# Two attention mixers of a transformer block, each written as one interleaved program

## The reference

```
h = rms_norm_2(x, n1)
proj = h @ w_in_l
qa, ka, va, qd, kd, vd, qc, kc, vc = jnp.split(proj, cuts, axis=-1)
qa = rms_norm_2(heads(qa, H_NA), qg[0])          # 4 heads: neighbourhood, with a bias
ka = rms_norm_2(heads(ka, H_NA), kg[0])
out_a = neighbourhood_attention(qa, ka, heads(va, H_NA), rpb_l, na_idx, na_dr, na_dc)
qd = partial_rotary(rms_norm_2(heads(qd, H_DIL), qg[1]), cos1, sin1)   # 6 heads: dilated
kd = partial_rotary(rms_norm_2(heads(kd, H_DIL), kg[1]), cos1, sin1)
out_d = dilated_window_attention(qd, kd, heads(vd, H_DIL), dil_idx, dil_val)
qc = axial_rotary(rms_norm_2(heads(qc, H_GQ), qg[2]), cos_r, sin_r, cos_c, sin_c)  # 6 heads on 2: grouped
kc = axial_rotary(rms_norm_2(heads(kc, H_GKV), kg[2]), cos_r, sin_r, cos_c, sin_c)
out_c = gqa_block_attention(qc, kc, heads(vc, H_GKV))
mix = jnp.concatenate([rms_norm_2(out_a, og[:NA_W]), rms_norm_2(out_d, og[NA_W:NA_W + DIL_W]),
                       rms_norm_2(out_c, og[NA_W + DIL_W:])], axis=-1)
return x + mix @ w_out_l
```

## Time and profile before

| | us |
|---|---|
| median of 3 runs | 1798.05 (1797.01 to 1801.28) |
| the profiled execution | 1802.4 |
| its span, first to last instruction | 1800.6 |
| TensorE busy | 1683.3 |
| VectorE busy | 1024.3 |
| ScalarE busy | 844.1 |
| GpSimd busy | 152.2 |

### The profile page before, as it was taken

The page is one execution under the profiler, slowest core; times in us unless marked ns, Lnnn a source line. Parts: engine busy times, 40 slices in busy tenths (PEclk is TensorE's granted clock), DMA queues, the critical chain, the costliest instruction groups (busy, mean ns, idle before and its releaser), DMA issues.

```text
span 1800.6 us, 28794 instructions
## 1 busy us (share of the span) xinstructions
PE 1683.3 (93%) x11689; PEld 1526.4 (85%) x11689; DVE 1024.3 (57%) x1303; ACT 844.1 (47%) x1185; POOL 152.2 (8%) x190
## 2 busy tenths in 40 slices
PE   7999997899999999998999998968999997899998
PEld 7999885799989999886689997946999987579997
DVE  6444555544455444668654445675655566666654
ACT  5344465444435443436544444564544454644443
POOL 0000011000000000230000002530000038000000
PEclk9999997999999999999999999989999998999999
DMA  7555441355545555432045555511545564025452
GB/s 267 187 186 187 162 153 61 133 194 186 186 164 188 185 181 181 154 118 71 25 176 187 183 179 139 201 48 47 187 166 197 182 180 163 1 100 190 177 188 92
DMA packets 40546, 276.85 MB, mean 154 GB/s; under 512 B 5505, under 2 KB 6290, under 8 KB 7570
## 3 DMA queue, kind: packets, MB, share of 16 engines
q1 hardware_dynamic: 39010, 271.00, 42.5%
q0 software_dynamic: 1456, 4.72, 1.7%
HBM read 274.65 MB, written 1.05 MB: 153 GB/s over the span
## 4 chain that ended last, share of the span: by engine, by line
PE 80%; DVE 9%; ACT 5%; POOL 3%; issue 2%; DMA 0%; SPq 0%; POOLq 0%; DVEq 0%; ACTq 0%
PE bank L661 19%; PE bank L642 14%; PE bank L644 14%; PE bank L643 14%; PE bank L622 5%; PE bank L573 3%; PE bank L574 3%; PE bank L575 3%; DVE w_lo L1356 2%; ACT prob L1178 1%; POOL proj L500 1%; ACT work L1064 1%; DVE prob L1536 1%; PE bank L718 1%; ACT w_hi L1054 1%
## 5 line engine op out<-in xcount | busy, mean ns | idle before, releaser
L1356 DVE TENSOR_TENSOR w_lo<-raw,w_hi 128x2048 fp32r<-128x2048 f32 x255 | 587.4, 2308 | 533.9 <-ACT w_hi L1054 533.2
L1054 ACT ACTIVATE w_hi<-raw 128x2048 fp32r<-128x2048 f32 x255 | 487.3, 1917 | 552.2 <-PE bank L644 404.0
L642 PE MATMUL bank<-xt_hi,w_hi 128*128 128x256 f32 x2112 | 599.8, 284 | 5.7 <-DVE xt_lo L1388 5.7
L644 PE MATMUL bank<-xt_hi,w_lo 128*128 128x256 f32 x2112 | 598.2, 283 | 0.0
L643 PE MATMUL bank<-xt_lo,w_hi 128*128 128x256 f32 x2112 | 598.1, 283 | 0.0
L642 PEld LDWEIGHTS bank<-xt_hi,w_hi 128*128 128x128 f32 x2112 | 405.6, 192 | 9.4 <-issue 5.0
L643 PEld LDWEIGHTS bank<-xt_lo,w_hi 128*128 128x128 f32 x2112 | 405.7, 192 | 2.5
L644 PEld LDWEIGHTS bank<-xt_hi,w_lo 128*128 128x128 f32 x2112 | 405.7, 192 | 0.0
L661 PE MATMUL bank<-w_hi,h_hi 128*128 128x512 f32 x528 | 208.3, 395 | 0.2
L661 PE MATMUL bank<-w_hi,h_lo 128*128 128x512 f32 x528 | 208.5, 395 | 0.0
L661 PE MATMUL bank<-w_lo,h_hi 128*128 128x512 f32 x528 | 208.2, 394 | 0.0
(11 more groups left out here) (301 smaller groups left out, 1635.2 us busy)
## 6 DMA issues: line engine op xcount, KB each, us to landing
raw<-in_stream SPq DMA_DIRECT2D x255, 1024.0 KB, 4.9
work<-in_rpb POOLq DMA_DIRECT2D x32, 64.0 KB, 3.7
X<-in_x SPq DMA_DIRECT2D x2, 512.0 KB, 4.0
prob<-in_cmp_w POOLq DMA_DIRECT2D x1, 1024.0 KB, 5.3
O<-in_cmp_w POOLq DMA_DIRECT2D x1, 1024.0 KB, 7.0
out<-X SPq DMA_DIRECT2D x1, 1024.0 KB, 4.0
cst<-in_consts SPq DMA_DIRECT2D x1, 776.0 KB, 5.9
O<-in_final_gain POOLq DMA_DIRECT2D x1, 512.0 KB, 4.2
```

The costliest lines, as they stand in the source:

```text
L642: pe.matmul(o, w_hi[:, sl, cols], xt_hi[:, k, :], start=(k == 0), stop=False)
L644: ins = pe.matmul(o, w_lo[:, sl, cols], xt_hi[:, k, :], start=False, stop=(k == KD - 1))
L1054: act.activation(w_hi[:, sl, :], raw[:, sl, :], ACT.Copy).then_inc(hi_done, 1)
L1356: dve.tensor_tensor(w_lo[:, sl, :], raw[:, sl, :], w_hi[:, sl, :].bitcast(F32), ALU.subtract).then_inc(lo_done, 1)
```

## The change

Each mixer becomes one function `sec_mixer` for each of three engines, in which the stages are interleaved by hand.

- The columns come as grouped, dilated, values of both, neighbourhood. TensorE takes the projection's units in halves of 24 matmuls and puts the attention of the grouped and then the dilated heads between them; steps of the output projection go between the jobs of the last pairs. The projection uses two banks, the output projection four (0 to 3), scores two, the transposed probabilities one, outputs and square sums one. The transposed probabilities have four places in SBUF.
- Sqrt and reciprocal become Ln and Exp with scale -0.5 on ScalarE, with the Newton step kept; the output norms get a Newton step too. The output norm is computed for each kind on its own, three square sums at a time.
- VectorE prepares the first token tile of the grouped and of the dilated heads, GpSimd the second, and both of the neighbourhood heads. GpSimd adds the mask after the dilated heads.
- The shared functions of the other stages lose their branches for the second block.

In the core of the diff, the first `sec_mixer` is TensorE's, the second ScalarE's, the third VectorE's; the last lines are GpSimd's.

```diff
 SEC_W = dict(qa=256, ka=256, va=256, qd=384, kd=384, vd=384, qc=384, kc=128, vc=128)
-SEC_ORDER = ("qa", "ka", "qd", "kd", "qc", "kc", "va", "vd", "vc")
-QA, KA, QD, KDL, QC, KC, VA, VD, VC = (sum(SEC_W[m] for m in SEC_ORDER[:i]) for i in range(9))
+SEC_ORDER = ("qc", "kc", "qd", "kd", "vc", "vd", "qa", "ka", "va")
...
+SEC_FT_BANK = (2, 3, 2, 3, 2, 4, 5)
...
+SEC_KINDS = ((QC, 8, 0, 1, 384), (QD, 12, 8, 4, 384), (QA, 8, 20, 8, 256))
+SEC_S, SEC_T, SEC_O = (4, 5), 6, 7
...
+            def sec_mixer(l):
...
+                def half(c, t):
+                    if t == 0:
+                        pe.wait_ge(lo_done, u0 + c + 1)
+                        if c >= 2:
+                            pe.wait_ge(pj_evac, p0 + c - 1)
+                    sl = (u0 + c) % NSPLIT
...
+                def transposes(g):
+                    if g == 0:
+                        pe.wait_ge(ft_ready_d, 4 + 2 * l)
+                        pe.wait_ge(ft_ready_p, 4 + 3 * l)
+                    elif g == 2:
+                        pe.wait_ge(ft_ready_d, 5 + 2 * l)
+                        pe.wait_ge(ft_ready_p, 5 + 3 * l)
+                        pe.wait_ge(ft_a, a0 + 1)
+                    elif g == 3:
+                        pe.wait_ge(ft_a, a0 + 2)
+                        pe.wait_ge(ft_d, d0 + 1)
+                    elif g == 4:
...
+                    if m in (0, 3, 6):
+                        pe.wait_ge(ft_a, a0 + (2, 3, 4)[m // 3])
+                        pe.wait_ge(ft_d, d0 + (1, 3, 4)[m // 3])
+                    if m == 6:
+                        pe.wait_ge(na_ready, l + 1)
+                    if m:
+                        pe.wait_ge(exp_done, 2 * (j0 + 2 * m))
+                    duo = [(jobs[i], bank[SEC_S[i % 2]]) for i in (2 * m, 2 * m + 1)]
...
+                def turn_p(i):
+                    pe.wait_ge(p_scaled, j0 + i + 1)
+                    if i:
+                        pe.wait_ge(pt_evac, j0 + i)
+                    for n, (qt, kt) in enumerate(pt_blocks(jobs[i])):
...
+                for c in range(5):
+                    half(c, 0)
+                    half(c, 1)
+                transposes(0)
+                transposes(1)
+                half(5, 0)
+                scores(0)
+                half(5, 1)
+                half(6, 0)
+                scores(1)
+                turn_p(0)
+                half(6, 1)
+                turn_p(1)
+                half(7, 0)
+                scores(2)
+                turn_p(2)
+                values(0)
+                turn_p(3)
+                half(7, 1)
+                transposes(2)
+                transposes(3)
+                half(8, 0)
+                transposes(4)
+                scores(3)
+                turn_p(4)
+                values(1)
+                turn_p(5)
+                half(8, 1)
+                scores(4)
+                turn_p(6)
+                values(2)
+                turn_p(7)
+                half(9, 0)
+                square_sums(0)
+                half(9, 1)
+                scores(5)
+                turn_p(8)
+                values(3)
+                turn_p(9)
+                out_k(0)
+                transposes(5)
+                transposes(6)
+                turn_p(10)
+                values(4)
+                turn_p(11)
+                scores(6)
+                out_k(1)
+                values(5)
+                scores(7)
+                square_sums(1)
+                turn_p(12)
+                out_k(2)
+                turn_p(13)
+                turn_p(14)
+                values(6)
+                turn_p(15)
+                out_k(3)
+                values(7)
+                square_sums(2)
+                out_k(4)
+                out_k(5)
+                out_last()
...
+            def sec_mixer(l):
...
+                def head_root(n):
+                    act.wait_ge(e_ms, 3 * l + n + 1)
+                    act.activation(head_rms(rstd, n), head_rms(ms, n), ACT.Ln).then_inc(e_ln, 1)
+                    act.wait_ge(e_ln, 3 * l + n + 1)
+                    act.activation(head_rms(rstd, n), head_rms(rstd, n), ACT.Exp, scale=-0.5).then_inc(e_rt, 1)
...
+                def out_root(kind):
+                    act.wait_ge(e_m, 3 * l + kind + 1)
+                    act.activation(o_norm[:, kind, :], o_ms, ACT.Ln).then_inc(e_ml, 1)
+                    act.wait_ge(e_ml, 3 * l + kind + 1)
+                    act.activation(o_norm[:, kind, :], o_norm[:, kind, :], ACT.Exp, scale=-0.5).then_inc(e_mr, 1)
...
+                evac(0)
+                split(u0 + 3)
+                evac(1)
+                head_squares(0)
+                split(u0 + 4)
+                head_root(0)
+                evac(2)
+                split(u0 + 5)
+                evac(3)
+                split(u0 + 6)
+                evac(4)
+                head_squares(1)
+                tiles(0)
+                tiles(1)
+                split(u0 + 7)
+                head_root(1)
+                exponentials(0)
+                evac(5)
+                split(u0 + 8)
+                turned(0)
+                exponentials(1)
+                evac(6)
+                turned(1)
+                split(u0 + 9)
+                turned(2)
+                exponentials(2)
+                turned(3)
+                pair_out(0)
+                evac(7)
+                tiles(3)
+                split(u0 + 10)
+                turned(4)
+                exponentials(3)
+                turned(5)
+                pair_out(1)
+                evac(8)
+                head_squares(2)
+                split(u0 + 11)
+                turned(6)
+                exponentials(4)
+                turned(7)
+                pair_out(2)
+                head_root(2)
+                evac(9)
+                split(u0 + 12)
+                out_root(0)
+                turned(8)
+                exponentials(5)
+                turned(9)
+                pair_out(3)
+                out_hi(0)
+                out_hi(1)
+                tiles(5)
+                turned(10)
+                turned(11)
+                pair_out(4)
+                exponentials(6)
+                out_hi(2)
+                pair_out(5)
+                split(u0 + 13)
+                turned(12)
+                out_root(1)
+                exponentials(7)
+                turned(13)
+                out_hi(3)
+                turned(14)
+                pair_out(6)
+                turned(15)
+                out_hi(4)
+                out_hi(5)
+                pair_out(7)
+                out_root(2)
+                out_hi(6)
+                out_hi(7)
+                split(u0 + 14)
...
+            def sec_mixer(l):
...
+                def newton(r, q, mean_sq, ins_sem):
+                    link(dve.tensor_tensor(q, r, r, ALU.mult))
+                    link(dve.tensor_tensor(q, q, mean_sq, ALU.mult))
+                    link(dve.tensor_scalar(q, q, -0.5, 1.5, ALU.mult, ALU.add))
+                    ins = dve.tensor_tensor(r, r, q, ALU.mult)
...
+                split(u0 + 3)
+                head_sums(0)
+                split(u0 + 4)
+                head_root(0)
+                sec_heads(dve, link, 0, 0, l, KT[:, 2048:2560])
+                dve.sem_inc(ft_ready_d, 1)
+                split(u0 + 5)
+                split(u0 + 6)
+                tiles(1)
+                head_sums(1)
+                split(u0 + 7)
+                head_root(1)
+                maxima(0)
+                scale(0)
+                maxima(1)
+                sec_heads(dve, link, 1, 0, l, KT[:, 2048:2560])
+                dve.sem_inc(ft_ready_d, 1)
+                split(u0 + 8)
+                scale(1)
+                split(u0 + 9)
+                maxima(2)
+                tiles(2)
+                scale(2)
+                split(u0 + 10)
+                tiles(4)
+                maxima(3)
+                scale(3)
+                head_sums(2)
+                maxima(4)
+                split(u0 + 11)
+                head_root(2)
+                scale(4)
+                out_mean(0)
+                maxima(5)
+                split(u0 + 12)
+                out_root(0)
+                out_scale(0)
+                out_scale(1)
+                scale(5)
+                out_lo(0)
+                out_scale(2)
+                out_lo(1)
+                tiles(6)
+                maxima(6)
+                out_lo(2)
+                scale(6)
+                split(u0 + 13)
+                maxima(7)
+                out_mean(1)
+                out_root(1)
+                out_scale(3)
+                scale(7)
+                out_scale(4)
+                out_lo(3)
+                out_scale(5)
+                out_lo(4)
+                out_lo(5)
+                out_mean(2)
+                out_root(2)
+                out_scale(6)
+                out_scale(7)
+                out_lo(6)
+                out_lo(7)
+                split(u0 + 14)
...
```

(50 more changed lines are left out.)

369 lines of the change are left out of this document (238 added, 131 removed).

## The result

The changed kernel takes 1817.2 us (median; 1815.1 to 1824.1) against 1798.3 us: a ratio of 1.0106, 95% interval 1.0079 to 1.0133. It is slower by 19 us. The forecast was 1808.7 us: right in sign, inside the range, 8.5 us too low.

The account below looks back on a forecast made before the run. TensorE, busy 93%, bounds it; 28 us a mixer of waits and clock were removable. New waits 25.3 + clock 7.3 = 32.6: +4.7 and +5.9 us, so 1798.05 + 10.6 = 1808.7 us; 8-in-10 range 1786 to 1820.

Parts of the forecast that it names:

- first transposes: TensorE's wait for GpSimd's first heads tile, prepared beside VectorE's: tile ready at 31.5 us, TensorE there at 29.1; 2.5 us.
- third job: Wait ahead of its transposes: VectorE's dilated tile, split and scalings, perhaps held by GpSimd's mask; 1.2 to 5.4, taken as 3.3 us.
- ninth and tenth job: Wait put at the tenth job, behind ScalarE's copies, split, two table loads and two passes: 3.9 us.
- first output matmul: Wait at the output projection's start, behind two exponentials, two scalings and the output tile's lower half: 3.9 us.
- fifteenth job: Wait for table loads and passes (3.4 us) and exponentials (1.8) under one output step of 2.7: 4.1 us.
- the later transfer: In the second mixer the transfer that the first roots need comes 1.2 us later, making that mixer +5.9 us.
- The clock: Half clock on TensorE after three or four new long waits, up to 2.8 us each, partly absorbed: 7.3 us a mixer.
- The clock holds: Rival: TensorE keeps full clock through the mixers, only waits remain, 5 us less than now a mixer, 1789 us; 23%.
- One table load serves Ln and Exp: Rival: ScalarE's roots need one load, tenth and fifteenth job come 2.6 us earlier, 1795 us; 8%.
- The interleaving costs more: Rival: coupled queues, whole 4.5 us mask, another clock fall (2.8), slower-draining loads; +11 us a mixer, 1820 us; 14%.
- The forecast case: The likeliest case over both mixers, 1800 to 1816 us by the ends of mask and clock; 45%.
- the stretched dilated tile: Sign named for being right: VectorE's tile of the dilated heads lasts longer where GpSimd's 4.5 us mask runs.

## Why the prediction was right in sign and 8 us short

**The mechanism held.** It said that the ceiling was 28 us of waits and clock a mixer, and that four coupled queues would lose more than that again. They lost 25.3 + 10.0 and 26.8 + 10.5 us. Of the 8.5 us that the forecast was too low, 4.1 lie in the mixers (6.3 and 8.4 us longer, not 4.7 and 5.9) and 3.4 behind them.

**The waits: 25.3 us predicted, 25.3 measured.** That the two agree to the tenth is luck; the sum is better than its terms:

| ahead of | predicted | measured |
|---|---|---|
| first transposes | 2.5 | 0 (and 0.95 behind them, for a split) |
| first and second scores | 0.7 | 0.31 + 0.45 |
| third job | 3.3 | 5.57 |
| fourth scores | 2.3 | 2.15 |
| eighth job, square sums | 2.5 | 1.58 + 0.34 |
| ninth and tenth job | 3.9 | 0.49 + 1.60 + 1.26 |
| first output matmul | 3.9 | 5.39 |
| fifteenth job | 4.1 | 3.90 |
| last place | 2.1 | 0.78 + 0.48 |

- First transposes: GpSimd began 20.3 us in (predicted 20.8) but took 8.7 us, not 10.7, and was done 29.0 us in, not 31.5. The two engines pay less for each other over a row of short instructions than I had read from the earlier trace rows.
- Third job: the step "if it holds VectorE off to its end, all of it counts; if not, nothing; I take the middle" was mis-sized. The earlier trace rows already showed a multiply that ended with GpSimd's (1.96 us long, 1.4 of them beside GpSimd's; no row shows the multiply of 1.40 us that the prediction names); that row decided the case, and the middle between two exclusive ends is a value that neither gives. The multiply lasted 4.84 us, some 4.2 more than the one before it.
- First output matmul: 1.5 us short. VectorE's split of 2.28 us started at 1203.06, 0.4 us after ScalarE's Exp was done, and the correcting passes behind it only at 1205.26.
- Second mixer: the later transfer was put at +1.2 us; the waits grew by 1.5.

**The clock: 7.3 us predicted, 10.0 and 10.5 measured.** This is the largest miss inside the mixers, 5.9 us; 2.3 us of it are made good, since the old mixers held 7.0 and 7.5 us of half clock (124.0 and 124.5 outside the waits) and not 6.1. I let each long wait cost 2.8 us and took off what the next wait absorbs. Shorter waits in a row count too: 0.49, 1.60 and 1.26 us ahead of the ninth to the tenth job left the values at 1.49 us and the next transposes at half clock, and the half clock then lasted through the 5.39 us wait and twelve output matmuls. The runs with filled waits show that the 10 us are clock: without their fillings they take 117 to 118 us in the first mixer.

**Behind the mixer: nothing predicted, 3.4 us measured.** The walk ended at the last output matmul. "SyncE's queue only waits for splits" was looked at; VectorE's order at the seam, split ahead of the update of X, was not.

**The rivals.** "The clock holds" is out: 0.90. With filled waits the clock did hold (0.99), but the time was 1802.6 us and not that rival's 1789. (The "even load of 76%" read for it is 78% in the earlier trace rows.) "One table load serves Ln and Exp" is out: two loads a root in all 12 roots. The Trainium skill's rule (ScalarE: Activation LUTs, section Table sets: the hidden batching unit) doesn't describe this program. The rival's price of 14 us for one load in two was not measured; leaving out 22 of the 24 loads came to 18, which by the load (0.8 us, an estimate) would be about 10 for 12 of them. "The interleaving costs more", with the whole mask and one more fall of the clock, to which I gave 14%, is the nearest to what happened: 1820 against 1817.2; no row shows its third part, loads that drain longer. The forecast case, to 1816, missed by a microsecond.

**The signs.** Of those named ahead, the 12 loads a mixer, the wait of 3.9 us ahead of the fifteenth job, the clock below 0.95 and the stretched dilated tile came true. The wait at the first output matmul, 5.4 us, was above the 3.5 to 4.5 named. GpSimd's first tile was 2.5 us early, and the tenth job waited 1.26 us, its wait spread over the two steps ahead of it.

## What to carry to other kernels

When work is interleaved so that TensorE never stands long, count for each handed-over result what stands ahead of it on its engine, table loads and correcting passes included: here 1.28 us loads and 0.42 us passes were worth 18 and 12 us. Keep GpSimd's long instructions where VectorE is idle: beside the 4.7 us mask a multiply of 0.6 us lasted 4.8. And where a wait can't be removed, filling it with matmuls that nobody reads keeps the clock, if they are shorter than the wait: it won 15 us here and 6 us in the old kernel, and cost 11 us where they were twice too long.

## What the runs showed of the hardware

- **GpSimd's power instruction** grows steeply: 0.55 us for 1 element a partition, 2.9 us for 16, 6.2 us for 24. For a tile of 256 it was not tried.
- **Scaling by a pointer** (one tensor input, 128x256) is held by GpSimd too: two of them 3.60 us beside the mask and 0.62 behind it.
- **The same code at two speeds.** In the eleven profiled kernels of the changed form the first mixer starts between 1105.7 and 1112.1 us, though nothing ahead of it differs. Between the kernels before and after, the largest difference, 4.9 us, arises from one norm to the next (206.18 to 344.67 us before, 207.53 to 341.15 after), by the granted clock (before, then after):

```profile
240.00:280.00 40.00, 36.62 (x244) 32.00 (x243) 20.78 (x32) 22.69 (x28) 0.00 (x0) 0.90 0.34 120
```

```profile
241.00:281.00 40.00, 36.61 (x261) 32.30 (x262) 20.78 (x32) 23.61 (x32) 0.00 (x0) 1.00 0.34 123
```

In 40 us with the same busy time TensorE did 244 matmuls at 0.90 and 261 at 1.00. Why the clock fell in one execution and not in the other stays open. A comparison of two profiled spans can be wrong by that much; comparing the stage that was changed is not.
